# A third buffer for gathered rows, their dots spread over other units, and scatters in another rhythm, in a fused attention and expert-layer block on one core

## The chip, the core and the metric

The kernel runs on one core of a Trainium2 chip. A core has a matrix engine (TensorE, PE in the profile), a vector engine (VectorE, DVE), a scalar engine (ScalarE, ACT), a general engine that also issues indirect transfers (GpSimd, POOL) and a queue engine that issues plain transfers (SyncE, SP). Sixteen DMA engines move the data of both. The metric is the time of one launch on the device, in microseconds (us), as the median of several runs.

## What is computed

One layer on 512 tokens of width 2048 in float32: a mixer (eight forgetting-attention heads, eight stick-breaking heads) and then an expert layer, in which each token picks 128 of 16,384 experts. The part that matters here is the expert layer:

```python
def peer_ffn(xn, w_pq, sub_keys, u, v):
    ...
    q = (xt @ w_pq).reshape(T, PEER_HEADS, 2, PEER_HALF)
    s = jnp.einsum('thcd,hcnd->thcn', q, sub_keys, ...)
    s1, i1 = lax.top_k(s[:, :, 0], PEER_TOPK)
    s2, i2 = lax.top_k(s[:, :, 1], PEER_TOPK)
    cand = (s1[..., :, None] + s2[..., None, :]).reshape(T, PEER_HEADS, PEER_TOPK * PEER_TOPK)
    ...
    top_s, pos = lax.top_k(cand, PEER_TOPK)
    idx = jnp.take_along_axis(cidx, pos, axis=-1)
    g = jax.nn.softmax(top_s, axis=-1).astype(xn.dtype)
    ...
        ub = u[ib]
        h = jax.nn.gelu(jnp.einsum('ted,td->te', ub, xb), approximate=False)
        vb = v[ib]
        return jnp.einsum('te,ted->td', gb * h, vb)
```

So for each token: 128 rows of `u` are dotted with the token, passed through gelu, multiplied by the 128 gates, and weigh 128 rows of `v`.

## The kernel before

**Dense and sparse tokens.** For most tokens the kernel does not gather. It multiplies all of `u` with the tokens (128 blocks of 128 experts), and later multiplies by a dense gate array that is zero where an expert was not chosen. The tokens are in four blocks of 128 (`TB`). The last block (`DB` = 3) is done wholly by gathers, in the later part of the program. Of block 2, the last 32 tokens (`PT`) and the 16 before them (`PB`) are taken out of the dense product, so that it has a width of 336 columns (`UT`). Their dots with the chosen rows of `u` are the *pair rows* of this change. The 32 tokens times 128 slots are 4096 rows, which make `PN` = 32 gathers of 128 rows of 2048 elements (1 MB); the 16 tokens make `NB` = 16 more.

**The stage.** The prologue has 68 units, numbered k = 0 to 67 (`N_PROUNITS`). Each unit is one block of 128 experts: SP loads 1 MB of `u` into `raw` (L412), ACT copies it to `wh` with rounding (`split_hi`, L420), DVE subtracts to get the rest `wl` (`lo`, L1187), and PE runs 48 matmuls of 336 columns (`gemm`, L440 to L442). ACT then takes the sum out with gelu (L1088), and SP stores it (L668). `raw`, `wh` and `wl` have two buffers each, so the load for unit k+2 waits until `lo` of unit k has run. DVE runs `lo` of unit k+1 in its own step k, first of all things in the step. PE cannot begin a unit before `lo` of that unit.

**What else runs in it.** On DVE, in this order within its step k: `lo`, a one-hot build (`hot`, L1528 and L1541, from step 31 on), a table lookup (`lookup`, L1492 to L1499, four steps for each block of tokens, times in `LOOK_AT`), the dots of pair rows (`pair_dot`, L1566) whose unit in `DOT_UNITS` is k, and other small pieces. From unit 32 (`GATE_FROM`) to 63, PE also runs two gate batches of four small matmuls in each unit (`gate_batch`, L2045), ACT takes them out into `gate_piece` (the first 4096 columns of `arena`), and SP stores this every four units (L699).

**The pair rows.** POOL issues for j = 0 to 47 a gather of 128 rows of `u` (L857) into `pair_rows[j % 2]`, once dot j-2 has run (the semaphore `pair_used`), and behind it a few scatters (`scatter_gate`, L843) which put single gates of block 0 into the dense gate array in memory. There are 128 scatters, and `behind[j]` of them follow gather j; each sixteenth waits until all earlier ones have landed. 52 of them stand behind the last gather. DVE's `pair_dot(j)` waits until gather j has landed, and everything behind it on DVE waits with it. After dot 31, SP copies the 16 tokens into `pair_x` (L686), and after the last dot the results are passed to the gates (`pair_weights`, which must be ready before PE's `turn_pair` ahead of unit 56, `PAIR_TURN`).

**After the prologue** follow 15 groups of eight units and a tail. There each unit still loads 1 MB, and the gathers of token block 3 run in three buffers (L874), with a dot or a weighted sum on DVE for each.

## Time and profile before

| | us |
|---|---|
| median of 3 runs | 3255.59 |
| lowest and highest | 3253.79 and 3257.19 |
| the profiled execution | 3256.15 |
| its span in the trace | 3254.4 |

PE is busy for 98% of the span, DVE 67%, ACT 33%, POOL 37%. The profile lists for each engine how long it was busy, how long it sat idle and what ended the idle time; time during which PE waits in a stage in which PE is otherwise without gaps is time of the whole program. The granted clock of PE is listed per stretch as a share of full speed. In timelines, the first two columns are the start and the length of a piece in us, and the bracket at the end is the idle time of that engine just before it and who ended it.

### The profile page before, as it was taken

How to read it: one execution, taken by the hardware profiler on the slowest of the kernel's cores; microseconds unless marked ns; L12 is line 12 of the kernel's file. 1: busy time of each engine (PE TensorE's matmuls, PEld its weight loads, DVE VectorE, ACT ScalarE, POOL GpSimd, SP SyncE). 2: the span in 40 equal slices, each digit the busy share in tenths (PEclk: the TensorE clock that was granted, in tenths of full speed). 3: DMA queues.
4: the chain of work that ended last, by engine and by line, in shares of the span. 5: the costliest groups of instructions: out<-in, count | busy, mean ns of one | idle time of the engine just before them, and what ended most of it. 6: DMA issues, size and time to landing. Idle time of an engine off the chain costs nothing. (4 is left out here: it accounts for less than half of the span.)

```text
span 3254.4 us, 40279 instructions
## 1 busy us (share of the span) xinstructions
PE 3193.3 (98%) x16407; PEld 2795.1 (86%) x16407; DVE 2190.4 (67%) x2514; ACT 1062.6 (33%) x1060; POOL 1209.4 (37%) x555
## 2 busy tenths in 40 slices
PE   8999999999999998889999999999999999999999
PEld 6887777888878898889999889889989988888887
DVE  3016665113037886667775898888888888888887
ACT  4123333444232232236653232323223322222221
POOL 4433333323433325665684233323323331223212
PEclk9999999999999999989999999999999999999999
DMA  4332222223342257888887989899988998888888
GB/s 150 112 109 88 88 88 88 72 88 114 132 142 97 89 181 271 289 257 272 262 235 272 351 338 344 340 345 345 365 320 332 364 338 314 320 336 340 342 321 318
DMA packets 177973, 778.21 MB, mean 239 GB/s; under 512 B 32944, under 2 KB 83248, under 8 KB 92976
## 3 DMA queue, kind: packets, MB, share of 16 engines
q1 hardware_dynamic: 115648, 457.77, 39.0%
q0 software_dynamic: 62208, 318.86, 27.1%
q8 instruction: 76, 1.25, 0.2%
q14 instruction: 41, 0.34, 0.0%
HBM read 731.10 MB, written 44.40 MB: 238 GB/s over the span
## 5 line engine op out<-in xcount | busy, mean ns | idle before, releaser
L440 PE MATMUL bank<-xh,wh 128*128 128x336 f32 (+1 forms) x2928 | 1009.2, 345 | 32.9 <-DVE wl L1187 32.9
L420 ACT ACTIVATE wh<-raw 128x2048 fp32r<-128x2048 f32 x343 | 656.1, 1913 | 1051.9 <-PE bank L467 859.1
L442 PE MATMUL bank<-xh,wl 128*128 128x336 f32 (+1 forms) x2928 | 995.3, 340 | 0.0
L441 PE MATMUL bank<-xl,wh 128*128 128x336 f32 (+1 forms) x2928 | 994.1, 340 | 0.0
L1187 DVE TENSOR_TENSOR wl<-raw,wh 128x2048 fp32r<-128x2048 f32 x252 | 576.9, 2289 | 222.6 <-ACT wh L420 222.5
L426 POOL TENSOR_TENSOR wl<-raw,wh 128x2048 fp32r<-128x2048 f32 x92 | 424.5, 4614 | 721.9 <-ACT wh L420 721.8
L440 PEld LDWEIGHTS bank<-xh,wh 128*128 128x128 f32 x2928 | 555.9, 190 | 71.2 <-DVE wl L1187 31.2
L441 PEld LDWEIGHTS bank<-xl,wh 128*128 128x128 f32 x2928 | 556.2, 190 | 35.2 <-issue 1.9
L442 PEld LDWEIGHTS bank<-xh,wl 128*128 128x128 f32 x2928 | 555.1, 190 | 35.1
L465 PE MATMUL bank<-wh,xh 128*128 128x512 f32 x1328 | 516.9, 389 | 0.0
L467 PE MATMUL bank<-wh,xl 128*128 128x512 f32 x1328 | 516.6, 389 | 0.0
L466 PE MATMUL bank<-wl,xh 128*128 128x512 f32 x1328 | 516.6, 389 | 0.0
L874 POOL DMA_INDIRECT arena<-in_u_rows,g_idx x128 | 247.4, 1932 | 454.2 <-DVE acc L1681 227.6
L874 POOL DMA_INDIRECT arena<-in_v_rows,g_idx x128 | 179.7, 1404 | 605.8 <-DVE acc L1681 314.6
L1660 DVE CUSTOM_DVE_ANT_0 arena<-arena 128x2048 f32<-128x2048 f32 x128 | 291.9, 2288 | 55.5 <-DMA arena<-in_u_rows,g_idx 55.3
L1681 DVE SCALAR_TENSOR_TENSOR acc<-arena,acc 128x2048 f32<-128x2048 f32 x128 | 300.5, 2348 | 3.5 <-DMA arena<-in_v_rows,g_idx 0.2
L465 PEld LDWEIGHTS bank<-wh,xh 128*128 128x128 f32 x1328 | 249.3, 188 | 51.9
L466 PEld LDWEIGHTS bank<-wl,xh 128*128 128x128 f32 x1328 | 249.3, 188 | 51.6
L467 PEld LDWEIGHTS bank<-wh,xl 128*128 128x128 f32 x1328 | 249.3, 188 | 51.5
L843 POOL DMA_INDIRECT gate_scratch<-arena x128 | 264.6, 2067 | 57.1 <-issue 37.2
L465 PE MATMUL bank<-wh,gh 128*128 128x512 f32 x720 | 280.6, 390 | 0.9 <-DVE wl L1187 0.9
L467 PE MATMUL bank<-wh,gl 128*128 128x512 f32 x720 | 280.3, 389 | 0.0
(219 smaller groups left out, 2866.3 us busy)
## 6 DMA issues: line engine op xcount, KB each, us to landing
raw<-in_u SPq DMA_DIRECT2D x128, 1024.0 KB, 5.5
raw<-in_v SPq DMA_DIRECT2D x128, 1024.0 KB, 7.3
raw<-in_w_in SPq DMA_DIRECT2D x56, 1024.0 KB, 5.1
arena<-gate_scratch SPq DMA_DIRECT2D x32, 768.0 KB, 9.1
raw<-in_w_out SPq DMA_DIRECT2D x16, 1024.0 KB, 5.1
raw<-in_w_pq SPq DMA_DIRECT2D x16, 1024.0 KB, 4.8
gate_scratch<-arena SPq DMA_DIRECT2D x8, 2048.0 KB, 9.8
act_scratch<-arena SPq DMA_DIRECT2D x68, 168.0 KB
```

Source lines behind the costliest of these rows:

```text
L420: nc.scalar.activation(wh[s][:], raw[s][:], ACT.Copy).then_inc(hi_done, 1)
L426: nc.gpsimd.tensor_tensor(wl[s][:], raw[s][:], wh[s][:].bitcast(F32), ALU.subtract).then_inc(lo_done, 1)
L440: nc.tensor.matmul(dst, w_h[:, c], xh[:, c, 0:width], start=(c == 0), stop=False)
L441: nc.tensor.matmul(dst, w_h[:, c], xl[:, c, 0:width], start=False, stop=False)
L442: last = nc.tensor.matmul(dst, w_l[:, c], xh[:, c, 0:width], start=False, stop=(c == KC - 1))
L465: nc.tensor.matmul(bank[:], a_hi(e)[:, rows_], w_h[:, e], start=begin, stop=False)
L466: nc.tensor.matmul(bank[:], a_hi(e)[:, rows_], w_l[:, e], start=False, stop=False)
L467: mm = nc.tensor.matmul(bank[:], a_lo(e)[:, rows_], w_h[:, e], start=False, stop=end)
L874: nc.gpsimd.indirect_dma_start(out=rows_g[n % ROW_BUFS], out_offset=None, in_=table, in_offset=bass.IndirectOffsetOnAxis(ap=g_idx[:, slot: ...
L1187: nc.vector.tensor_tensor(wl[k % 2][:], raw[k % 2][:], wh[k % 2][:].bitcast(F32), ALU.subtract).then_inc(lo_done, 1)
L1660: nc.vector.tensor_tensor_reduce(out=rows_g[b], in0=rows_g[b], in1=x_tok, scale=1.0, scalar=0.0, op0=ALU.mult, op1=ALU.add, accum_out=dots ...
L1681: nc.vector.scalar_tensor_tensor(out=acc[:, DB, :], in0=rows_g[b], scalar=dots[:, GM + j:GM + j + 1], in1=acc[:, DB, :], op0=ALU.mult, op1 ...
```

## The change

There are three edits, in the stage just described.

1. **A third buffer.** The first 24 pair-row gathers go in turn to three buffers, the new one being columns 2048 to 4095 of `arena`; from gather 24 on there are two, as before. `PAIR_BUF[j]` is the buffer, `PAIR_TURN_OF[j]` its use number, `PAIR_BEFORE[j]` the gather that had it before. A gather now waits for the dot of `PAIR_BEFORE[j]`. ACT waits for dot 23 before it writes `gate_piece`, which covers the third buffer.
2. **Other units.** The second lookup (block 1) moves from steps 24 to 27 to the steps 14, 18, 22 and 26, and the dots move to steps without a lookup. Units of the dots before and after: 2 and 3 in step 12, against 2 in 12 and 3 and 4 in 13; dots 2 to 21 in steps 12 to 23 before, dots 2 to 16 there now; dots 24 to 31 two in each of steps 28 to 31 before, dots 22 to 27 in steps 28 to 31 now and dots 28 to 31 one each in steps 33 to 36. The dots of the 16 tokens (32 to 47) were in steps 33 to 51 and are in 38 to 52. So the steps of SP and ACT that hang on dot 31 and dot 47 come at step 37 instead of 32, and at 53, 55 and 57 instead of 52, 54 and 56.
3. **Scatters.** Behind gathers 4 to 31 stand one and two scatters in turn (42 in all) instead of one, one and two (39 behind gathers 3 to 31), and 49 behind the last gather instead of 52.

```diff
-LOOK_AT = {0: 8, 1: 24, 3: 56}
+LOOK_AT = {0: (8, 9, 10, 11), 1: (14, 18, 22, 26), 3: (56, 57, 58, 59)}
...
-DOT_UNITS = sorted([9, 11] + list(range(12, 24)) + [12, 14, 15, 17, 18, 20, 21, 23] + [24, 26] +
-                   2 * list(range(28, 32)) + [_k for _k in range(33, 52) if _k not in (36, 41, 46)])
+DOT_UNITS = sorted([9, 11, 12, 13, 13, 15, 15, 16, 17, 17, 19, 19, 20, 21, 21, 23, 23, 24, 25, 25, 27, 27, 28, 28,
+                    29, 30, 30, 31] + list(range(33, 37)) + list(range(38, 53)) + [45])
+PAIR_BUF = [_j % 3 if _j < 24 else _j % 2 for _j in range(PN + NB)]
...
-        pair_rows = [acc[:, 1 + b, :] for b in range(2)]
+        pair_rows = [acc[:, 1, :], acc[:, 2, :], at(D, D)]
...
-            behind = [0] * 3 + [1 + (_j % 3 == 0) for _j in range(3, PN)] + [2 + _j % 2 for _j in range(NB - 1)]
+            behind = [0] * 4 + [1 + _j % 2 for _j in range(4, PN)] + [2 + _j % 2 for _j in range(NB - 1)]
...
-                if j >= 2:
-                    pool.wait_ge(pair_used, j - 1)
+                if PAIR_BEFORE[j] >= 0:
+                    pool.wait_ge(pair_used, PAIR_BEFORE[j] + 1)
...
+                        if b == 0:
+                            act.wait_ge(pair_used, max(_j for _j in range(PN) if PAIR_BUF[_j] == 2) + 1)
...
-                dve.wait_ge(pair_gathered[j % 2], 16 * (j // 2 + 1))
+                rows_j = pair_rows[PAIR_BUF[j]]
+                dve.wait_ge(pair_gathered[PAIR_BUF[j]], 16 * (PAIR_TURN_OF[j] + 1))
```

**Order on DVE, steps 12 to 14.** A `TENSOR_TENSOR` into `wl` is `lo`; each dot is two `ISA` rows (the product and sum, and its read-out); `arena<-arena,acc` is a dot from the third buffer. Before:

```order
L1187 TENSOR_TENSOR wl0<-raw0,wh0 128x2048
L1566 ISA acc,arena<-acc 128x2048
L1566 ISA arena 128x1
L1566 ISA acc,arena<-acc 128x2048
L1566 ISA arena 128x1
L1187 TENSOR_TENSOR wl1<-raw1,wh1 128x2048
L1566 ISA acc,arena<-acc 128x2048
L1566 ISA arena 128x1
L1187 TENSOR_TENSOR wl0<-raw0,wh0 128x2048
L1566 ISA acc,arena<-acc 128x2048
L1566 ISA arena 128x1
L1566 ISA acc,arena<-acc 128x2048
```

After (line numbers are those of the changed kernel):

```order
L1192 TENSOR_TENSOR wl0<-raw0,wh0 128x2048
L1572 ISA arena<-arena,acc 128x2048
L1572 ISA arena 128x1
L1192 TENSOR_TENSOR wl1<-raw1,wh1 128x2048
L1572 ISA acc,arena<-acc 128x2048
L1572 ISA arena 128x1
L1572 ISA acc,arena<-acc 128x2048
L1572 ISA arena 128x1
L1192 TENSOR_TENSOR wl0<-raw0,wh0 128x2048
L1497 TENSOR_TENSOR gl<-arena,iota16 128x1024
L1500 TENSOR_TENSOR gl<-gl,arena 128x1024
L1504 TENSOR_REDUCE arena<-gl 128x64
```

Between two `lo` there stood up to two dots in nearly every step; now a step with one dot, one with two, and one with the lookup and no dot follow each other.

**Order on DVE, steps 30 and 31**, where the third buffer is no longer in use. Before, from `lo` of unit 31 (two dots in each step):

```order
L1187 TENSOR_TENSOR wl0<-raw0,wh0 128x2048
L1566 ISA acc,arena<-acc 128x2048
L1566 ISA arena 128x1
L1566 ISA acc,arena<-acc 128x2048
L1566 ISA arena 128x1
L1187 TENSOR_TENSOR wl1<-raw1,wh1 128x2048
L1528 TENSOR_TENSOR gh<-iota128,arena 128x512
L1536 TENSOR_SCALAR arena<-arena 128x128
L1566 ISA acc,arena<-acc 128x2048
L1566 ISA arena 128x1
```

After, from `lo` of unit 31 (dots 25 and 26, then 27):

```order
L1192 TENSOR_TENSOR wl0<-raw0,wh0 128x2048
L1572 ISA acc,arena<-acc 128x2048
L1572 ISA arena 128x1
L1572 ISA acc,arena<-acc 128x2048
L1572 ISA arena 128x1
L1192 TENSOR_TENSOR wl1<-raw1,wh1 128x2048
L1533 TENSOR_TENSOR gh<-iota128,arena 128x512
L1541 TENSOR_SCALAR arena<-arena 128x128
L1572 ISA acc,arena<-acc 128x2048
L1572 ISA arena 128x1
L1524 COPY arena<-bank 128x384
```

One dot has left step 31; step 30 still has two.

**Order on POOL, from the gathers 2 and 3 on**, `L857` and `L860` being gathers and `L843` and `L846` scatters. Before:

```order
L857 DMA acc<-in_u_rows,arena 128x2048 [waits pair_used] x2
L843 DMA gate_scratch<-arena 6291456x1 [waits gwt_done,placed,gates_zeroed]
L843 DMA gate_scratch<-arena 6291456x1
L857 DMA acc<-in_u_rows,arena 128x2048 [waits pair_used]
L843 DMA gate_scratch<-arena 6291456x1
L857 DMA acc<-in_u_rows,arena 128x2048 [waits pair_used]
L843 DMA gate_scratch<-arena 6291456x1
L857 DMA acc<-in_u_rows,arena 128x2048 [waits pair_used]
L843 DMA gate_scratch<-arena 6291456x1 x2
```

After:

```order
L860 DMA arena<-in_u_rows,arena 128x2048
L860 DMA acc<-in_u_rows,arena 128x2048 [waits pair_used] x2
L846 DMA gate_scratch<-arena 6291456x1 [waits gwt_done,placed,gates_zeroed]
L860 DMA arena<-in_u_rows,arena 128x2048 [waits pair_used]
L846 DMA gate_scratch<-arena 6291456x1 x2
L860 DMA acc<-in_u_rows,arena 128x2048 [waits pair_used]
L846 DMA gate_scratch<-arena 6291456x1
L860 DMA acc<-in_u_rows,arena 128x2048 [waits pair_used]
L846 DMA gate_scratch<-arena 6291456x1 x2
```

The third gather has no wait now and goes to `arena`, and two scatters stand behind every second gather.

## Rows read from the trace of the kernel before

**Rows 1.** The page, busy time of the engines.
```profile
PE 3193.3 (98%) x16407; PEld 2795.1 (86%) x16407; DVE 2190.4 (67%) x2514; ACT 1062.6 (33%) x1060; POOL 1209.4 (37%) x555
```

**Rows 2.** Waits of PE: engine, line, released by: us in total, times, longest.
```profile
PE bank L440 <- DVE wl L1187: 32.9, 11, 6.4
```

**Rows 3.** Stretches: length; busy PE, PEld, DVE, ACT, POOL; PE clock; DMA share; GB/s.
```profile
1240.00:1300.00 60.00, 49.00 (x294) 48.08 (x292) 34.17 (x27) 13.52 (x12) 41.83 (x25) 0.91 0.85 297
1300.00:1360.00 60.00, 48.29 (x290) 46.70 (x288) 34.27 (x26) 14.80 (x14) 42.56 (x23) 0.94 0.83 285
...
sum 210.00, PE 172.16 PEld 168.60 DVE 134.85 ACT 50.03 POOL 142.33; mean PE 34.43 PEld 33.72 DVE 26.97 ACT 10.01 POOL 28.47
```

**Rows 4.** Timeline of ACT: L1088 starts when PE ends a unit.
```profile
1233.50 0.45 ACT L1088 ACTIVATE arena<-bank 128x336 f32<-128x336 f32 x1 [5.10 <-PE bank L442]
...
1240.86 0.45 ACT L1088 ACTIVATE arena<-bank 128x336 f32<-128x336 f32 x1 [5.11 <-PE bank L442]
1241.21 1.91 ACT L420 ACTIVATE wh<-raw 128x2048 fp32r<-128x2048 f32 x1
...
1447.37 0.45 ACT L1088 ACTIVATE arena<-bank 128x336 f32<-128x336 f32 x1 [12.01 <-PE bank L442]
...
1475.17 0.45 ACT L1088 ACTIVATE arena<-bank 128x336 f32<-128x336 f32 x1 [0.66 <-PE bank L442]
...
1484.35 0.45 ACT L1088 ACTIVATE arena<-bank 128x336 f32<-128x336 f32 x1 [4.97 <-PE bank L442]
```

**Rows 5.** Timeline of DVE: two `lo` with two late dots between, and a lookup.
```profile
1254.43 2.29 DVE L1187 TENSOR_TENSOR wl<-raw,wh 128x2048 fp32r<-128x2048 f32 x1
1261.20 2.29 DVE L1566 CUSTOM_DVE_ANT_0 acc<-acc 128x2048 f32<-128x2048 f32 x1 [4.49 <-DMA acc<-in_u_rows,arena]
...
1266.30 2.29 DVE L1566 CUSTOM_DVE_ANT_0 acc<-acc 128x2048 f32<-128x2048 f32 x1 [2.80 <-DMA acc<-in_u_rows,arena]
...
1268.52 2.29 DVE L1187 TENSOR_TENSOR wl<-raw,wh 128x2048 fp32r<-128x2048 f32 x1
...
1371.90 1.22 DVE L1492 TENSOR_TENSOR gl<-arena,iota 128x1024 fp32r<-128x1024 f32 x1
```

**Rows 6.** Timeline of POOL in the same stretch, and one scatter that waited.
```profile
1250.37 2.81 POOL L857 DMA_INDIRECT acc<-in_u_rows,arena  x1 [1.50 <-DVE arena L1566]
...
1256.26 1.33 POOL L857 DMA_INDIRECT acc<-in_u_rows,arena  x1 [0.30 <-issue]
...
1407.51 1.57 POOL L843 DMA_INDIRECT gate_scratch<-arena  x1 [4.13 <-DMA gate_scratch<-arena]
```

**Rows 7.** DMA from 1250 to 1440: packets, MB, engine share; issues to landing, us.
```profile
q0 software_dynamic: 9529, 29.87, 45.3%
q1 hardware_dynamic: 5472, 23.19, 35.3%
...
raw<-in_u SPq DMA_DIRECT2D x19, 1024.0 KB, 5.3
...
gate_scratch<-arena POOLq DMA_INDIRECT x38
acc<-in_u_rows,arena POOLq DMA_INDIRECT x28, 8.3
```

**Rows 8.** DMA from 1610 to 1735, where POOL issues 48 scatters alone.
```profile
q0 software_dynamic: 7243, 0.25, 11.8%
```

**Rows 9.** A stretch of the later groups, columns as in rows 3.
```profile
2100.00:2300.00 200.00, 200.00 (x1078) 181.36 (x1078) 175.19 (x106) 57.92 (x45) 61.71 (x39) 1.00 0.92 350
```

**Rows 10.** POOL's last gather and last scatter, and the queue engine behind it.
```profile
1602.09 1.21 POOL L857 DMA_INDIRECT acc<-in_u_rows,arena  x1 [1.65 <-DVE arena L1566]
...
1735.93 3.29 POOL L843 DMA_INDIRECT gate_scratch<-arena  x1 [0.30 <-issue]
...
1754.04 0.33 SPq L412 DMA_DIRECT2D raw<-in_u  x1
```

**Rows 11.** Start of unit 54 by ACT, and the end of `pair_weights` on DVE.
```profile
1640.29 0.45 ACT L1088 ACTIVATE arena<-bank 128x336 f32<-128x336 f32 x1 [0.71 <-PE bank L442]
...
1647.73 0.29 DVE L1581 TENSOR_TENSOR arena<-arena 64x128 f32<-64x128 f32 x1
```

More of the change, by code:

```diff
@@ L382, in build @@
         pair_chosen = sem("pair_chosen")
-        pair_gathered = [sem(f"pair_gathered{b}") for b in range(2)]
+        pair_gathered = [sem(f"pair_gathered{b}") for b in range(3)]
         pair_used = sem("pair_used")
@@ L1613, in _ @@
                 for t in LOOK_AT:
-                    if LOOK_AT[t] <= k < LOOK_AT[t] + 4:
-                        lookup(t, (k - LOOK_AT[t]) // 2, (k - LOOK_AT[t]) % 2)
-                if k == LOOK_AT[0] + 3:
+                    if k in LOOK_AT[t]:
+                        lookup(t, LOOK_AT[t].index(k) // 2, LOOK_AT[t].index(k) % 2)
+                if k == LOOK_AT[0][-1]:
                     place()
```

12 lines of the change are left out of this document (7 added, 5 removed).

## The prediction

> **What bounds the kernel now.** I read the page first. PE is busy for 98% of the span [rows 1], so the program is as long as PE's work plus PE's gaps, and another engine matters only where PE waits for it. Then the waits of PE. Only one of them is long and lies in the stage of the change: 32.9 us, in 11 pieces, before the first matmul of a unit, released by DVE's `lo` [rows 2]. Then the stretches of that stage. From 1240 to 1450 PE is busy for 172.2 of 210 us and its granted clock is between 0.78 and 0.94 of full speed [rows 3]; later, in the main groups, it is busy for 200 of 200 at 1.00 [rows 9]. So time is lost in two ways, and I count both at once by the length of the units. ACT's L1088 marks the end of a unit. An undisturbed unit is 1240.86 - 1233.50 = 7.36 us, one with gate batches 1484.35 - 1475.17 = 9.18. Units 13 to 32 run from 1240.86 to 1447.37 [rows 4], which is 206.5 us; without a disturbance they would take 19 x 7.36 + 9.18 = 149.0. The loss is **57.5 us**: 210 - 172.2 = 37.8 idle, the rest clock. All other units of the prologue that I looked at have their undisturbed length within a few tenths.
>
> Why `lo` is late stands in DVE's timeline. Between the `lo` at 1254.43 and the next at 1268.52 lie two dots that waited 4.49 and 2.80 us for their gathers [rows 5]. POOL's timeline gives the round trip: the gather issued at 1250.37 was used at 1261.20, the one of 1256.26 at 1266.30, so 10 to 11 us from issue to use [rows 5, 6]. A buffer's cycle is then about 0.3 (dot to issue) + 10 + 2.3 (dot) = 12.6 us. With two buffers that is a dot each 6.3 us, but the old table asks for 20 dots in the 12 units 12 to 23, one each 88.3 / 20 = 4.4 us.
>
> **The change, part by part.** *Third buffer with the new units.* Three buffers allow a dot each 12.6 / 3 = 4.2 us. The new table asks for 26 dots in the 20 units 12 to 31, one each 147.2 / 26 = 5.7. Does each step fit on DVE? `lo` can start 2.35 after its unit's start (L1088 and L420 on ACT [rows 4]) and DVE needs about 2.2 to 2.3 for `lo` and for each dot [rows 5]. A step with two dots ends at 2.3 + 3 x 2.2 = 9.0, which is 1.6 into the next unit, and the next `lo` may begin as late as 5.1 into it. So a two-dot step bears some 3.4 us of waiting for gathers before PE notices, a one-dot step 5.6. A lookup step has no dot: 2.3 + 2.2 + 3 x 1.25 = 8.3 [rows 5], which fits. Walking through the steps with these numbers and with POOL's mean of (41.83 + 42.56) / 48 = 1.76 us for an instruction [rows 3] plus its gap of 0.3 [rows 6], no dot before 23 waits longer than 1.7 us, and nothing reaches PE.
>
> The end of the three-buffer part is different. Count from the start of unit 28. Gather 23 starts near 0 (after dot 20), and dot 23 waits until 9.9, ends 12.1. Gather 24 starts at 5.9, behind 23 and two scatters, and dot 24 ends at 18.2, with `take_slots` at 18.8. Gather 25 starts at 10.0. Gather 26 needs the buffer of dot 24 (two buffers now) and also stands behind scatter 32, the one that waits for all earlier scatters; such a wait was 4.1 us at 1407.51 [rows 6]. It starts at 19.7 and lands at 29.7. In step 30 `lo` runs to 21.1, dot 25 to 23.4, and dot 26 waits 6.3 us and ends at 32.0. So `lo` of unit 32 ends at 34.2 where PE wants it at 29.4: **about 5 us are left**. The same walk through the old table gives 54 us of lateness, against 57.5 measured, which is why I trust it.
>
> *DMA load.* Take shares of 16 engines. From 1250 to 1440, q1 used 35.3% of 190 us for 19 units, 3.53 us a unit; q0 used 45.3%, 86.1 us, for 28 gathers and 38 scatters [rows 7]. A scatter is 11.8% of 125 us / 48 = 0.31 [rows 8], so a gather is (86.1 - 11.7) / 28 = 2.66. Units 12 to 31 now need 20 x 3.53 + 23 gathers (5 to 27) x 2.66 + 35 scatters x 0.31 = 142.6 us in 147.2, or 97%. The later groups run at a share of 0.92 with PE never waiting [rows 9]; at such a share the 142.6 take 155, which is 8 us too long. The stretch now runs at 0.83 to 0.85 [rows 3], with pauses since the gathers wait for buffers. Between 5 (no crowding) and 8 to 9 (a share of 0.92), I take **8 us left**, nearer to the loaded end, since the rows of the later groups are the ones with three buffers.
>
> *Clock.* The clock was 1.00 where PE had no gaps [rows 9] and lower only where it had. It is inside the 57.5 and goes with it; with 5 us of stall left some of it stays, inside the 8.
>
> *Scatters and the tail.* POOL has 49 scatters behind the last gather instead of 52, but that gather comes one unit later. The 52 took from 1603.3 to 1739.2 [rows 10], 2.6 us each; so the tail ends, seen from the units, 9.2 - 3 x 2.6 = 1.4 us later. SP's load behind it was issued at 1754.04 [rows 10], and that was due to `lo`; 15 us of cover, 13.6 now: nothing. All of it shifts with the units, as it hangs on dots.
>
> *Steps that move on SP and ACT.* `pair_weights` ended 1647.73 + 0.3 - 1640.29 = 7.7 us into unit 54 [rows 11]; the same work in unit 55 must be done at its end, 9.2, where PE's `turn_pair` now waits for it: 1.4 us of cover, and if it fails, as much is lost as it is late; I take 0, bound 2. The copy of the 16 tokens (eight small transfers) comes at SP's step 37, behind a 2 MB gate store, and is wanted a unit later: 0, bound 2. ACT's new wait is for dot 23 (step 28) at step 33: 0.
>
> Sum: 57.5 - 8 = 49.5 us gained. The profiled execution had 3256.15, so 3206.7; the median of the runs is 0.6 below it: **3206**. Nothing behind the prologue changes, as its groups start from the same order of events.
>
> Two rules of the Trainium skill can be set beside this. Rows first: a gather's landing took 8.3 us in the median [rows 7]. The skill's page "DMA: Bandwidth & Descriptors", section "Anatomy of one DMA — SWDGE (gpsimd) path", fits 2.0 us plus bytes / 436e3 us, an estimate of 4.4 us for 1 MB. By that a third buffer would hardly be needed and the loss would be some 14 us, not 57.5; the measured landing decides. If that is what an unloaded gather takes, the other 4 us are queueing, which more gathers in flight may lengthen: the second case below. And the gather that started within `lo` took 2.81 us on POOL, one beside it 1.33 [rows 6]. "SBUF — State Buffer", section "Who interferes with whom", infers that a `tensor_tensor` doesn't hold up descriptor generation; the row speaks against that. By the page POOL would be some 2 us less late; the sum has the measured mean.
>
> **The rivals.** *Forecast* (0.66): 2 to 15 us left, 3199 to 3214; the low end is 57.5 with only 2 left, the high end 8, the two bounds of 2 of the moved steps and 3 for one more late step.
>
> *DMA or POOL is full* (0.19): at the share seen now, 0.85, the 142.6 us take 168, 20 too long; with the stall of 5 that leaves 15 to 28: 3214 to 3227. For it: 97% is more than any long row shows, and POOL's 2.5 instructions for each dot are 5.2 us of 5.7. Against: gathers 24 to 27 are all that must be on time at the end, and three early gathers are a reserve.
>
> *The third buffer gives nothing* (0.09): say gathers of one queue are served strictly one behind the other, so that the cycle stays at 12.6 for two. The new units alone then leave stalls of about 5 us in each group of four units (19, 23, 27) and 5 + 2 + 5 in 30 to 32, with small ones some 33 us, at a trip of 11 us 43: 3230 to 3241. Against: in the later groups 350 GB/s are moved with three buffers of the same kind [rows 9].
>
> *The stall is not the dots* (0.03), and PE waits again for late loads of `u`: loads landed in 5.3 us [rows 7] and have some 10; within 0.2%.
>
> *Slower* (0.03): the tail of scatters becomes what starts the main groups. Dense gathers fill POOL, the prologue is 49.5 us shorter, and if scatters slow from 2.6 us to over 4.0 each, 49 of them eat the cover of 13.6 and the gain and 6.5 more: 3262 and up. The tail's rate was steady in its two rows, so little.
>
> **How the numbers follow.** A measurement of this kernel can tell 0.2%, 6.5 us. The range goes from the forecast's low end to nearly the end of the second case, 3199 to 3226; about 0.85 lies within, and leaving out the second case would leave 0.34 out. Faster is the first three cases, 0.94; same 0.03; slower 0.03.
>
> **What would show it.** In the changed profile units 13 to 31 should be 7.36 long and PE's wait before L443 a few us, nearly all at unit 32 (and perhaps 30), released by `lo`, with DVE waiting for gather 26. The clock from 1240 on should be 1.00 but near that place. DMA share there should be 0.9 or more, and landing of gathers 9 to 12 us. Landing over 12, or stalls at 15, 19, 23 and 27, would be the second or third case; a wait before `turn_pair`, or of SP for `scattered` ahead of the main groups, would show that moved steps had no cover.

## The result

The changed kernel takes 3228.18 us (median of 4 runs, 3225.24 to 3236.83) against 3255.61 for the kernel before: a ratio of 0.9918 with an interval of 0.9906 to 0.9931. That is 27 us faster. The forecast was 49.5 us faster, with a range that ended at 3226, so the result lies 2 us outside it. The direction was right; almost half of the expected gain is missing. Section by section below, "loss" is counted as in the prediction: the length of a stretch of units, read from ACT's L1091 (L1088 before), less 7.36 us for each plain unit and 9.175 for each with gate batches.

The profiled execution took 3236.83 us, the slowest of the four. The page's line of busy times, which answers to [rows 1]:

```profile
PE 3188.1 (99%) x16407; PEld 2791.3 (86%) x16407; DVE 2189.6 (68%) x2514; ACT 1062.4 (33%) x1060; POOL 1233.8 (38%) x555
```

Waits of PE over the whole program (engine, line, released by: us in total, times, longest), as [rows 2]. The wait for `lo` fell from 32.9 to 18.0 us, and one for the one-hot build ahead of a gate batch rose from 3.8 us to 6.7:

```profile
PE bank L443 <- DVE wl L1192: 18.0, 5, 6.4
...
PE bank L2051 <- DVE arena L1546: 6.7, 2, 3.7
```

Stretches of the stage, columns as in [rows 3] (length; busy PE, PEld, DVE, ACT, POOL; clock; DMA share; GB/s). The last row is the start of the main groups:

```profile
1240.00:1300.00 60.00, 60.00 (x393) 60.00 (x392) 51.02 (x38) 18.05 (x16) 51.01 (x24) 1.00 0.95 329
1300.00:1360.00 60.00, 57.78 (x368) 57.50 (x367) 45.21 (x35) 18.05 (x16) 48.92 (x26) 0.97 0.95 318
1360.00:1410.00 50.00, 42.61 (x271) 42.03 (x271) 32.73 (x37) 14.09 (x18) 35.05 (x17) 0.93 0.86 285
...
1500.00:1550.00 50.00, 46.28 (x313) 46.00 (x312) 35.18 (x54) 26.56 (x42) 41.05 (x17) 0.97 0.79 252
1550.00:1600.00 50.00, 47.00 (x318) 46.72 (x316) 36.89 (x58) 27.72 (x38) 40.33 (x17) 0.97 0.92 286
1731.20:1800.00 68.80, 60.42 (x310) 55.24 (x309) 43.98 (x29) 18.65 (x15) 15.86 (x12) 0.93 0.88 333
```

The first 60 us, where PE lost 11 us and its clock was 0.91 before, now run without a gap at 1.00, as forecast. POOL is busy there for 51.01 of 60 us in 24 instructions. With 0.3 us ahead of each, that is 58 of 60: **POOL is full**. The gaps of PE lie in three other places. ACT's timeline gives their size, as [rows 4] (the ends of units 12, 32 and 67, then ACT's first copy of the main groups, which waited for its load):

```profile
1243.20 0.46 ACT L1091 ACTIVATE arena<-bank 128x336 f32<-128x336 f32 x1 [5.10 <-PE bank L445]
...
1406.66 0.45 ACT L1091 ACTIVATE arena<-bank 128x336 f32<-128x336 f32 x1 [5.61 <-PE bank L445]
...
1731.14 0.45 ACT L1091 ACTIVATE arena<-bank 128x336 f32<-128x336 f32 x1 [5.28 <-PE bank L445]
1735.99 1.92 ACT L423 ACTIVATE wh<-raw 128x2048 fp32r<-128x2048 f32 x1 [4.40 <-DMA raw<-in_u]
```

Units 13 to 32 took 1406.66 - 1243.20 = 163.5 us, a loss of 14.5 (57.5 before): 4.0 at unit 27 and 10.5 in units 28 to 32. Units 33 to 67 lost 10.6 (1.4 before). From the end of unit 67 (1762.64 before) to the end of the span it is 3235.1 - 1731.14 = 1504.0 us, against 3254.4 - 1762.64 = 1491.8. With 2.3 us that unit 12 ended later (1243.20 against 1240.86; unit 0 was already that late, and no other profile shows it), the difference of the two profiled executions is 43.0 - 9.2 - 12.2 - 2.3 = 19.3 us, which is 3256.15 - 3236.83. In a second profile of the same kernel (a_rep, 3231.78) it is 41.3 - 7.5 - 9.5 + 0.1 = 24.4.

**Place one, units 27 to 32.** Unit 27 is late through dot 19, which still has three buffers. POOL's gather 19, then its dot and `lo` of unit 27 on DVE:

```profile
1335.04 1.94 POOL L860 DMA_INDIRECT acc<-in_u_rows,arena  x1 [0.30 <-issue]
```

```profile
1343.87 2.29 DVE L1572 CUSTOM_DVE_ANT_0 acc<-acc 128x2048 f32<-128x2048 f32 x1 [3.21 <-DMA acc<-in_u_rows,arena]
...
1346.09 2.28 DVE L1192 TENSOR_TENSOR wl<-raw,wh 128x2048 fp32r<-128x2048 f32 x1
```

Units 30 to 32 are late through dot 26. DVE's timeline: dots 25 and 26, then `lo` of unit 32.

```profile
1379.86 2.29 DVE L1572 CUSTOM_DVE_ANT_0 acc<-acc 128x2048 f32<-128x2048 f32 x1
...
1390.66 2.29 DVE L1572 CUSTOM_DVE_ANT_0 acc<-acc 128x2048 f32<-128x2048 f32 x1 [8.50 <-DMA acc<-in_u_rows,arena]
...
1392.88 2.29 DVE L1192 TENSOR_TENSOR wl<-raw,wh 128x2048 fp32r<-128x2048 f32 x1
```

POOL's timeline there: gather 25, scatters 31 and 32 (the latter waits until all earlier ones have landed, as at 1407.51 in [rows 6]), gathers 26 and, one scatter further, 27.

```profile
1369.83 2.67 POOL L860 DMA_INDIRECT acc<-in_u_rows,arena  x1 [0.30 <-issue]
1372.80 2.48 POOL L846 DMA_INDIRECT gate_scratch<-arena  x1 [0.30 <-issue]
1382.70 1.56 POOL L846 DMA_INDIRECT gate_scratch<-arena  x1 [7.42 <-DMA gate_scratch<-arena]
1384.57 1.00 POOL L860 DMA_INDIRECT acc<-in_u_rows,arena  x1 [0.30 <-issue]
...
1387.75 1.00 POOL L860 DMA_INDIRECT acc<-in_u_rows,arena  x1 [0.30 <-issue]
```

Dot 26 is late, as the prediction said, but its gather was used 6.1 us after its start (1384.57 to 1390.66). It was late because it started late, behind a wait for landing of 7.42 us where the walk had 4.1. Counted as in the walk, from the start of unit 28 (1357.56 here), gather 25 started at 12.3 instead of 10.0 and gather 26 at 27.0 instead of 19.7. Of these 7.3 us, 3.3 are the longer wait, 2.3 the later gather 25, and the rest longer instructions between them. Its buffer had been free since 1377.1, the end of dot 24.

**Place two, units 46 to 48.** Again DVE (two dots in step 45, the second waiting 7.90 us) and POOL (its gather at 1519.62):

```profile
1521.84 2.29 DVE L1572 CUSTOM_DVE_ANT_0 acc<-acc 128x2048 f32<-128x2048 f32 x1
...
1532.04 2.29 DVE L1572 CUSTOM_DVE_ANT_0 acc<-acc 128x2048 f32<-128x2048 f32 x1 [7.90 <-DMA acc<-in_u_rows,arena]
```

```profile
1513.91 3.54 POOL L846 DMA_INDIRECT gate_scratch<-arena  x1 [0.30 <-issue]
1517.76 1.56 POOL L846 DMA_INDIRECT gate_scratch<-arena  x1 [0.30 <-issue]
1519.62 2.58 POOL L860 DMA_INDIRECT acc<-in_u_rows,arena  x1 [0.30 <-issue]
1522.50 3.07 POOL L846 DMA_INDIRECT gate_scratch<-arena  x1 [0.30 <-issue]
1525.88 1.56 POOL L846 DMA_INDIRECT gate_scratch<-arena  x1 [0.30 <-issue]
...
1533.13 2.67 POOL L846 DMA_INDIRECT gate_scratch<-arena  x1 [4.38 <-DMA gate_scratch<-arena]
```

The buffer was free at 1515.91 (the dot of 1513.69 and its read-out), POOL came to the gather 3.7 us later, and its rows were used after 12.4 us.

**Place three, the start of the main groups.** POOL's longest wait for landing, its last scatter, the first instruction behind the wait for all of them, and SP's load for the second main unit, which waits for the same (1754.04 in [rows 10]):

```profile
1653.09 2.42 POOL L846 DMA_INDIRECT gate_scratch<-arena  x1 [12.55 <-DMA gate_scratch<-arena]
...
1727.01 2.61 POOL L846 DMA_INDIRECT gate_scratch<-arena  x1 [0.30 <-issue]
1731.15 0.26 POOL L870 MEMSET arena<- 128x192 f32 x1 [1.53 <-DMA gate_scratch<-arena]
```

```profile
1731.16 0.33 SPq L415 DMA_DIRECT2D raw<-in_u  x1
```

Before, that load went out 8.6 us ahead of the end of unit 67. Now it leaves with that end, 0.01 us after the row in which POOL goes on because all scatters have landed, and PE waits twice in 1700 to 1800, 8.4 us in all.

### The profile page after: what moved, and what is told of

The parts are those of the page before. It is cut to its first block, busy times and chain, and to the rows that moved or that the text cites. A ratio compares the mean times of both kernels' runs of the same rounds, so it can differ in the third digit from the quotient of the medians.

```text
span 3235.1 us, 40279 instructions
## 1 busy us (share of the span) xinstructions
PE 3188.1 (99%) x16407; PEld 2791.3 (86%) x16407; DVE 2189.6 (68%) x2514; ACT 1062.4 (33%) x1060; POOL 1233.8 (38%) x555
## 4 chain that ended last, share of the span: by engine, by line
PE 89%; DMA 4%; POOL 3%; DVE 1%; ACT 1%; issue 1%; SPq 0%; ACTq 0%; DVEq 0%
PE bank L468 14%; PE bank L469 14%; PE bank L470 14%; PE bank L443 14%; PE bank L445 14%; PE bank L444 14%; POOL gate_scratch L846 3%; DMA raw<-in_u 1%; PE bank L2051 1%; PE bank L1882 1%; DMA gate_scratch<-arena 1%; POOL acc L860 1%; PE bank L1863 1%; DMA acc<-in_u_rows,arena 1%; PE bank L1927 1%
## 5 line engine op out<-in xcount | busy, mean ns | idle before, releaser
L443 PEld LDWEIGHTS bank<-xh,wh 128*128 128x128 f32 x2928 | 553.9, 189 | 54.9 <-DVE wl L1192 11.1
L846 POOL DMA_INDIRECT gate_scratch<-arena x128 | 287.0, 2242 | 78.1 <-DMA gate_scratch<-arena 41.3
```

What stands on the lines that cost most here:

```text
L443: nc.tensor.matmul(dst, w_h[:, c], xh[:, c, 0:width], start=(c == 0), stop=False)
L846: nc.gpsimd.indirect_dma_start(out=gate_cells, out_offset=bass.IndirectOffsetOnAxis(ap=where[:, j:j + 1], axis=0), in_=best[:, 0].rearrang ...
```

## The experiments

All times are medians of four runs or more, and each ratio is to the kernel before, run in the same set. The theory after the first profile: the third buffer and the new units do what they should, and what is left comes from POOL, whose queue of gathers and scatters is full. Rivals: the two-buffer round trip of gather 26 (the prediction's step), DMA engines that are full, the dots of the 16 tokens being too close by themselves, and, for the start of the main groups, the 3 MB reload of `acc`.

This table has the readings of all profiles (one for each kernel), worked out as above: losses in units 13 to 32 and 33 to 67, how long before the end of unit 67 the last scatter started, and the time from that end to the span's end ("rest"). "Late" is how much later than in the kernel before the fourth unit of the main groups ended, counted from the end of unit 67. It is the part of "rest" that the start of the main groups costs. The time of before is from its set in the first row, and it was 3256.6 to 3258.3 in the other four.

| kernel | median us | 13 to 32 | 33 to 67 | last scatter | late | rest |
|---|---|---|---|---|---|---|
| before | 3255.6 | 57.5 | 1.4 | 26.7 | 0 | 1491.8 |
| changed | 3228.2 | 14.5 | 10.6 | 4.1 | 12.8 | 1504.0 |
| a_rep | 3231.2 | 16.2 | 8.9 | 13.9 | 4.7 | 1501.3 |
| b_buf | 3238.2 | 34.1 | 0.1 | 26.7 | 0.0 | 1494.5 |
| c_units | 3250.4 | 31.5 | 10.2 | 4.1 | 12.0 | 1504.1 |
| d_noscat | 3205.2 | 0.7 | 0.1 | | 0.0 | 1499.6 |
| e_oldscat | 3224.4 | 4.9 | 8.6 | 4.1 | 12.6 | 1508.4 |
| f_buf27 | 3226.7 | 15.9 | 8.3 | 14.0 | 5.2 | 1497.8 |
| g_scatmove | 3216.6 | 6.9 | 8.2 | 14.0 | 4.4 | 1496.3 |
| h_both | 3215.2 | 5.1 | 8.9 | 12.3 | 4.6 | 1500.5 |
| k_thin | 3227.1 | 8.3 | 2.8 | 1.3 | 14.7 | 1507.6 |
| l_late | 3225.6 | 9.2 | 6.0 | 1.1 | 14.4 | 1508.4 |
| m_poolbusy | 3202.2 | 7.9 | 0.6 | | 0.0 | 1492.9 |
| n_tail8 | 3220.9 | 15.0 | 7.9 | 32.3 | 0.0 | 1492.9 |

The two last columns don't always go together. In d_noscat the main groups begin on time, and yet "rest" is 7.8 us longer than before; in a_rep, e_oldscat and h_both some 4 to 5 us of it aren't late starts. That time is lost inside the main groups. In d_noscat its largest piece stands at the very end:

```profile
3150.00:3203.90 53.90, 47.02 (x195) 37.97 (x193) 39.04 (x25) 7.76 (x5) 9.24 (x6) 0.93 0.78 287
```

In the last 53.9 us of the kernel before PE was busy for 50.54 at a clock of 0.99. What causes this loss stays open.

### The changed kernel again

> The changed kernel once more, unaltered, for a second trace. Theory A, three fixed places: the loss of some 37 us that the first trace shows (units 27 and 30 to 32: 14.5; units 46 to 48: 10.4; the start of the main groups behind the last scatters: 12.3) comes from the order of the work, so a second trace shows a loss at the same three places, each within about 5 us, and the ratio to before is 0.989 to 0.994. Theory B, chance: the places differ from run to run (transfers that collide by chance), so that at least one of the three is gone and the time is nearer to 3225 than to 3237.

Measured: 3231.24 us (3224.22 to 3237.18), ratio 0.9918 [0.9894, 0.9943]. The losses are much the same: 5.1 at units 25 and 27 (behind dots 16 and 19, which waited 5.52 and 6.17 us), 11.1 in units 28 to 32, 8.9 about unit 46. Only the start of the main groups differs more than the 5 us allowed (4.7 us late instead of 12.8), with a last scatter that came 10 us earlier.

### One edit at a time: the buffer, the units

b_buf keeps the old units, lookups and scatters and has the third buffer alone. c_units has the new units with two buffers and the old scatters. In c_units:

```diff
-PAIR_BUF = [_j % 3 if _j < 24 else _j % 2 for _j in range(PN + NB)]
+PAIR_BUF = [_j % 2 for _j in range(PN + NB)]
```

> The third buffer alone: the old units of lookups and dots, the old rhythm of scatters. Theory A (a buffer's round trip of 12.6 us bounds the dots): the walk through the steps leaves 25 to 29 us of lateness in units 13 to 32 instead of 57.5, so 3224 to 3232 if nothing is lost behind it, and up to 12 more where the last scatters reach the main groups. Rival C (the third buffer gives nothing, gathers of one queue are served one behind the other): 3250 to 3257.

> The new units of lookups and dots alone: two buffers and the old rhythm of scatters. Theory A: with a trip of 10 to 11 us the walk leaves 33 to 43 us in units 13 to 32, with stalls of about 5 us at 19, 23, 27 and 30 to 32: 3231 to 3241 and a little more for the tail. Rival C: the units are the whole of the change, so this one is as fast as the changed kernel, 3225 to 3230.

Measured: b_buf 3238.22 us, ratio 0.9943 [0.9926, 0.9961]; c_units 3250.44, 0.9971 [0.9957, 0.9985]. Of the 57.5 us in units 13 to 32, the buffer alone takes 23.4, the units alone 26.0, both together 43.0, and both with the old scatters (e_oldscat, below) 52.6. Each half is worth something, and neither makes up for the other. This refutes the rival "the third buffer gives nothing": without it the new units keep 31.5 us of loss, with it 14.5, and b_buf is far from that rival's 3250 to 3257. Both expectations missed in part: b_buf kept 34.1 us instead of 25 to 29, and c_units kept less than the 33 to 43 expected but took 9 us more than 3241, since nothing had been counted for units 33 to 67 and too little for the tail. The other columns tell what the new units cost: the loss of some 10 us in units 46 to 51 and the late start of the main groups come with the new units even at the old scatter rhythm (c_units), and are absent without them (b_buf). So c_units gains 26 us and gives back about 21.

### No scatters

The 128 scatters and all waits for them are left out (the gates of token block 0 stay zero).

```diff
-                for slot in range(sum(behind[:j]), sum(behind[:j + 1])):
-                    scatter_gate(slot)
...
-            pool.wait_ge(scattered, 16 * SLOTS)
```

> The changed kernel without the 128 scatters and without the waits for them; the gates of token block 0 stay zero, so this work is left out. Theory A (POOL, whose scatters stand ahead of gathers, makes the dots late at units 27, 30 to 32 and 46 to 48, and the last scatters hold up the main groups): the loss at 46 to 48 and at the main groups goes, and that at 27 to 32 falls to 5 or less: 3198 to 3206. Rival B2 (the DMA engines are full at those places; a scatter is only 0.3 us of them): units 27 to 32 and 46 to 48 still lose some 20 us together and only the start of the main groups is mended: 3212 to 3218.

Measured: 3205.22 us (3203.93 to 3206.28), ratio 0.984 [0.9823, 0.9856]. The stretches of d_noscat:

```profile
1240.00:1400.00 160.00, 160.00 (x1056) 159.97 (x1055) 131.72 (x113) 55.35 (x62) 55.37 (x27) 1.00 0.89 339
1500.00:1600.00 100.00, 100.00 (x700) 100.00 (x699) 76.12 (x122) 63.07 (x94) 8.94 (x8) 1.00 0.77 273
```

PE has no gap in the prologue, at 339 GB/s against 329 and 318 in the changed kernel. So gathers, loads of `u` and dots fit, and the losses of the prologue and the late main groups hang on the scatters. A DMA share that is full by gathers and loads is refuted. That the time is the predicted one (3205.2, forecast 3206) is luck: the prologue lost 0.8 us where the forecast had left 8, and the main groups lost 7.8 us where it had nothing.

### POOL busy, but nothing moved

Each scatter is replaced by four fills of 128x512 on POOL, one after the other (again the gates of block 0 stay zero).

```diff
-                    scatter_gate(slot)
+                    for step in range(4 * slot, 4 * slot + 4):
+                        if step:
+                            pool.wait_ge(pool_step, step)
+                        nc.gpsimd.memset(gl[:, 1024:1536].bitcast(F32), 0.0).then_inc(pool_step, 1)
```

> The changed kernel with each of its 128 scatters replaced by four fills of 128 x 512 numbers on POOL, one after the other, which keep POOL busy for about 2.1 to 2.6 us, nearly as long as a scatter (2.24 us and a gap of 0.3), but move nothing; the gates of token block 0 stay zero, and nothing waits for landed scatters. It stands between the changed kernel (3228 to 3231, losses 14 to 16 in units 13 to 32 and 9 to 11 in 33 to 67) and d_noscat (3205, losses 0.7 and 0.1). If POOL's issue time alone is what makes the gathers late, the losses should be 8 to 16 and 5 to 10, and the time 3218 to 3230. If the waits for landed scatters (3.8 to 12.6 us, seven of them) and the traffic of the scatters do it, the losses should be under 3 and 2, and the time 3205 to 3210.

Measured: 3202.19 us (3199.05 to 3207.04), ratio 0.9829 [0.9812, 0.9845]. The groups of POOL's fills in m_poolbusy and of its scatters in the changed kernel (busy us, mean ns | idle before them):

```profile
L870 POOL MEMSET gl<- 128x512 f32 x512 | 273.0, 533 | 26.9
```

```profile
L846 POOL DMA_INDIRECT gate_scratch<-arena x128 | 287.0, 2242 | 78.1 <-DMA gate_scratch<-arena 41.3 <-issue 36.9
```

The fills take 300 us with their gaps, the scatters 324 without their waits for landing, so POOL's load is nearly the same. The result falls between the two theories. In units 13 to 32 the loss is 7.9 us, all at unit 31: dot 26 waits 4.2 us, and its gather began straight behind fills. That is the 5 to 8 us which the prediction had for this place, and POOL's issue time accounts for it. In 33 to 67 it is only 0.6 us. The rest, some 7 us in 13 to 32 (the 4 to 5 at units 25 and 27 among it), 8 to 10 in 33 to 67, and the late main groups, needs what the fills don't have: the waits for landing (41.3 us in all) and scatters whose length goes up to 6.32 us. These two were not separated. Nor does the median show the 7.9 us, since it is 3 us below that of d_noscat. The two profiles say why that can be: m_poolbusy lost 7.8 us more in the prologue, but its main groups took 6.7 us less (1492.9 against 1499.6). Its profiled execution was also the longest of its four.

### A third buffer for longer

Gathers 24 to 26 stay in the turn of three, so gather 26 no longer waits for a dot two places ahead of it.

```diff
-PAIR_BUF = [_j % 3 if _j < 24 else _j % 2 for _j in range(PN + NB)]
+PAIR_BUF = [_j % 3 if _j < 27 else (_j - 27) % 2 for _j in range(PN + NB)]
```

> The changed kernel with the third buffer kept for gathers 24 to 26 too; from 27 on two buffers. Gather 26 then waits for dot 23 and not for dot 24. Theory A (the loss of some 10 us at units 30 to 32 is the round trip of gather 26 in two buffers): that stall goes to 3 us or less, the time falls by 6 to 10 us against the changed kernel. Rival A2 (gather 26 is late since POOL comes to it late, behind scatters and the wait at scatter 32): the stall stays at 7 us or more, and the time is within 3 us.

Measured: 3226.68 us (3223.91 to 3229.71), 0.9905 [0.9888, 0.9921], not to be told from the changed kernel. Its timelines of POOL and of DVE, at the same place:

```profile
1381.15 2.92 POOL L846 DMA_INDIRECT gate_scratch<-arena  x1 [5.45 <-DMA gate_scratch<-arena]
1384.37 1.01 POOL L860 DMA_INDIRECT arena<-in_u_rows,arena  x1 [0.30 <-issue]
```

```profile
1390.16 2.29 DVE L1572 CUSTOM_DVE_ANT_0 arena<-arena,acc 128x2048 f32<-128x2048 f32 x1 [7.52 <-DMA arena<-in_u_rows,arena]
```

Gather 26 now goes to the third buffer, starts at the same time as before, and its dot waits 7.52 us. The buffer was not what it waited for; the scatter ahead of it was, with its wait for landing. Units 28 to 32 lose 8.3 us instead of 10.5 and 11.1, so the two buffers are worth 3 us there at most. The prediction had both causes in its walk, and there too the scatter's wait ended last; but it took the change from three buffers to two for what makes this place different, and that is refuted. What the two buffers would do comes next in line: in g_scatmove, below, gather 26 waits 5.21 us for dot 24, whose buffer it takes.

### The scatters elsewhere

e_oldscat is the changed kernel with the old rhythm (edit 3 undone: 52 behind the last gather). g_scatmove takes six scatters away from gathers 23 to 27 and four from 34 to 46, and puts the ten behind 28 to 33, where POOL waits for dots; 79 stay ahead of the last gather. h_both is g_scatmove and f_buf27 together.

```diff
-            behind = [0] * 4 + [1 + _j % 2 for _j in range(4, PN)] + [2 + _j % 2 for _j in range(NB - 1)]
+            behind = [0] * 4 + [1 + _j % 2 for _j in range(4, 23)] + [0, 1, 0, 1, 0] + [3] * 5 + [6] + \
+                [3 if _j in (36, 42) else 2 for _j in range(34, PN + NB - 1)]
```

> The changed kernel with the old rhythm of scatters (39 behind gathers 3 to 31 and 52 behind the last, as before the change). The runs so far: without scatters the prologue loses nothing, with them 25 us, and some 5 to 12 more at the start of the main groups. Theory A2 (POOL is nearly full, so a few scatters more or less behind each gather only move the lateness about): within 4 us of the changed kernel either way, less late in units 27 to 32 by 1 or 2 us and the tail of scatters up to 8 us later, so more lost at the main groups. Rival (the rhythm is what carries the change): 8 us slower or more.

> The changed kernel with the same count of scatters ahead of the last gather (79) in another rhythm: 2 instead of 8 behind gathers 23 to 27, 21 instead of 11 behind gathers 28 to 33, where POOL sat idle, and 28 instead of 32 behind gathers 34 to 46. Theory A2 (POOL's queue is what makes the dots late): the stall at units 30 to 32 falls to about half and the one at 46 to 48 too, 6 to 12 us less than the changed kernel. Theory A (round trip in two buffers): the first stall stays, 0 to 4 us less.

> Both of the last two edits: the third buffer up to gather 26 and the moved scatters. Theory A and A2 together: units 13 to 37 lose 3 us or less, units 38 to 63 half of the 9 to 10 us, the main groups still 5 to 12: 3208 to 3218, faster than the changed kernel by 10 to 18 us. If one of the two theories is wrong, it is as the better one of the two single edits.

Measured: e_oldscat 3224.35 us (3217.91 to 3227.79), 0.9892 [0.9875, 0.9908]; g_scatmove **3216.57** (3211.26 to 3219.95), 0.9872 [0.9856, 0.9889]; h_both **3215.23** (3207.9 to 3219.92), 0.9863 [0.9846, 0.9879]. DVE of g_scatmove at dot 26 (the wait was 8.50), and PE's wait for `lo` in 1240 to 1410 (9.6 us in the changed kernel):

```profile
1381.71 2.29 DVE L1573 CUSTOM_DVE_ANT_0 acc<-acc 128x2048 f32<-128x2048 f32 x1 [2.94 <-DMA acc<-in_u_rows,arena]
```

```profile
PE bank L443 <- DVE wl L1193: 3.5, 1, 3.5
```

Moving these scatters by a few gathers about halves the loss in units 13 to 32, from 14.5 and 16.2 (15.0 in n_tail8) to 6.9 (8.3 and 9.2 in k_thin and l_late, which have the same scatters there), with buffers and units untouched. That is more than the 6 to 12 us expected of the whole. The loss in 33 to 67, which should have halved too, did not: 8.2 us, most of it at unit 41 instead of 46. The intervals of g_scatmove and h_both lie below both of the changed kernel; whether h_both is better than g_scatmove can't be told. Its time came as expected, its places didn't (5.1 us in 13 to 32 where 3 or less was expected, 8.9 behind them where half of that was). e_oldscat shows that edit 3 was no help to the dots: without it units 13 to 32 lose only 4.9 us, where 1 or 2 us less than the changed kernel had been expected. Three more scatters stand in its tail, but its main groups start no later than those of the changed kernel (12.6 us, against 12.8); another 4 us of its "rest" are lost inside the groups. The median is not to be told from the changed kernel.

### Units 46 to 48, and the tail

k_thin is g_scatmove with 20 instead of 28 scatters behind gathers 34 to 46, and so 57 behind the last. l_late is k_thin with the 3 MB reload of `acc` at SP's step 62 instead of 57. n_tail8 is the changed kernel with its last 8 scatters left out (their gates stay zero).

```diff
-                [3 if _j in (36, 42) else 2 for _j in range(34, PN + NB - 1)]
+                [1 if _j in (36, 38, 39, 40, 41, 42) else 2 for _j in range(34, PN + NB - 1)]
```

```diff
-                if k == DOT_UNITS[-1] + 5:
+                if k == 62:
```

```diff
-                for slot in range(sum(behind[:j]), sum(behind[:j + 1])):
+                for slot in range(sum(behind[:j]), min(sum(behind[:j + 1]), SLOTS - 8)):
```

> The kernel of g_scatmove with 20 scatters instead of 28 behind gathers 34 to 46, so that 57 instead of 49 stand behind the last gather. There is left a loss of 8 to 9 us at unit 41 or 46. Theory P: POOL is full there, since a dot's share of 1 gather and 2.2 scatters of 3 us takes as long as a unit; units 33 to 67 should then lose 3 us or less instead of 8.2. Rival D: the DMA engines are full there (share 0.97 in 1500 to 1580), or 16 dots in 15 units do not fit by themselves; then the 8 us stay. Price under either: 8 more scatters of 2.7 us in the tail, 21.6 us, less the 8 that the last gather comes earlier; the last scatter stood 14.0 us ahead of the end of unit 67, so it comes about with it, and the main groups may start some 5 us late. Total: P 3210 to 3218, D 3217 to 3226.

> The kernel of k_thin with SP's 3 MB reload of acc at step 62 instead of 57. In the profile of the changed kernel a wait of POOL for landed scatters was 12.55 us at 1653, behind that reload and a 2 MB gate store. Theory T: the reload holds the scatters' landing up; that wait should be 4 to 7 us, the last scatter 5 to 8 us earlier against the end of unit 67, and the main groups start without a gap (PE idle before the first main matmul under 2 us): 3205 to 3213. Rival: the gate store alone, or the collision of the reload with later waits, does it; the last scatter stands where it does in k_thin, and the time is that of k_thin within 3 us.

> The changed kernel with the last 8 of its 128 scatters left out (those experts' gates of token block 0 stay zero), so that 41 instead of 49 stand behind the last gather; everything ahead of that gather is as in the changed kernel. Theory: the last scatter starts the main groups, since SP's load for the second main unit waits until all have landed. In the changed kernel it was issued 4.1 and 13.9 us ahead of the end of unit 67 and the first main groups began 10.5 and 2.8 us late; in b_buf it was 26.7 us ahead and nothing was late. Here it should be 24 to 34 us ahead, the main groups begin within 0.5 us of their place and the program take 4 to 12 us less than the changed kernel, 3217 to 3226, with the losses in the prologue as they were (13 to 17 and 8 to 11 us). Rival: the main groups begin late for another reason (the 3 MB reload, late activations); then they are still 3 to 12 us late and the time is 3226 to 3232.

Measured: k_thin 3227.08 us (3224.31 to 3230.69), 0.9912 [0.9895, 0.9929]; l_late 3225.64, 0.9899 [0.9882, 0.9916]; n_tail8 3220.88 (3218.54 to 3221.55), 0.9883 [0.9867, 0.99].

k_thin: theory P's reading came in its profile (2.8 us instead of 8.2 in units 33 to 67), but l_late, with the same scatters, lost 6.0 there, all at unit 41 and ahead of the step that was moved. So thinning helped by 2 to 5 us in these profiles, and one profile doesn't tell how much. Rival D falls by d_noscat and m_poolbusy, which have the same dots and lose 0.1 and 0.6. The total missed: 3210 to 3218 was expected. The last scatter started 1.3 us before the end of unit 67, and the main groups began 14.7 us late instead of the "some 5" that I had allowed. A scatter taken out of the gathers' way is paid in the tail.

l_late: the time is as the rival said, that of k_thin within 3 us, and the last scatter comes at the same place (1.1). But the long wait moved with the reload. In k_thin the reload left at 1623.41, and the wait of 10.02 us began 10.4 us behind it. In l_late the wait about that place took 1.80 us, and the one of 11.08 us stands right behind the reload's new place. POOL, then SP, of l_late:

```profile
1639.74 1.55 POOL L846 DMA_INDIRECT gate_scratch<-arena  x1 [1.80 <-DMA gate_scratch<-arena]
...
1684.62 1.65 POOL L846 DMA_INDIRECT gate_scratch<-arena  x1 [11.08 <-DMA gate_scratch<-arena]
```

```profile
1671.93 0.43 SPq L698 DMA_DIRECT2D acc<-acc_scratch  x1
```

The other profiles agree. In the changed kernel, c_units and e_oldscat too, the wait that began 1 to 7 us behind the reload took 12.55, 10.91 and 10.88 us, and no other scatter behind the last gather waited over 7.5. In a_rep POOL came to it 2.8 us ahead of the reload, and it took 5.79: most of the 10 us by which a_rep's last scatter was earlier. So the reload does go with the long landing. Why landings take longer there stays open, and no run shows a reload placed where no group of scatters is waited for.

n_tail8 is the counterpart: the same losses in the prologue (15.0 and 7.9), but SP's load leaves 8.7 us ahead of the end of unit 67 at 1726.81, as in the kernel before, and the first main groups begin where they should, within 0.1 us. So the last scatters cause the late start. Its timeline of SP:

```profile
1718.08 0.33 SPq L415 DMA_DIRECT2D raw<-in_u  x1
```

How much cover the tail needs can be read from a_rep. Its last scatter started at 1714.80 and ran for 1.56 us, and then its POOL and SP had these rows:

```profile
1721.07 0.26 POOL L870 MEMSET arena<- 128x192 f32 x1 [4.72 <-DMA gate_scratch<-arena]
```

```profile
1721.08 0.33 SPq L415 DMA_DIRECT2D raw<-in_u  x1
```

The last scatter landed 4.7 us after its issue had ended, the load left 7.6 us ahead of the end of unit 67 (1728.70) instead of 8.6, and PE waited 2.9 us (with the clock that this costs, 4.7 us late).

A version with fewer waits for landing was not tried. Each such wait stands between two heads' gates, two heads can pick the same expert, and their scatters would then add to one cell while both are in flight.

## Why the prediction was right and wrong

- **What bounds the kernel, and the third buffer with the new units: right in the main.** Up to unit 26 the changed kernel lost nothing, in its first profile, and PE's clock went back to 1.00 there. Without scatters the prologue lost 0.8 us.
- **"No dot before 23 waits longer than 1.7 us, and nothing reaches PE" was wrong.** Dot 19 waited 3.21 us and unit 27 took 4.0 us more (in a_rep dots 16 and 19 waited 5.52 and 6.17, and units 25 and 27 took 5.1 us more). All profiles with new units, third buffer and scatters lose 4 to 8 us at these two units; d_noscat and m_poolbusy lose nothing there. The step behind it is POOL's queue, taken at its mean.
- **The term of the sum that failed: "8 us left" in units 13 to 32, which measured 14.5 and 16.2.** At the end of the three-buffer part place and dot were right (26, in step 30). The size was off, 10.5 and 11.1 us in units 28 to 32 where the walk had 5, and so was the weight of the causes: not the two-buffer round trip (f_buf27), but POOL's queue. Its issue time alone makes 7.9 us (m_poolbusy). The wait for landing ahead of scatter 32, taken at 4.1 us from the one row of such a wait [rows 6], measured 7.42, 6.27 and 5.45 in three profiles (2.43 in e_oldscat, where units 28 to 32 lost 0.9). I had one row for it and took it as the value, though it varies by 5 us. That the 8 us had been raised from 5 for a crowded DMA brought the number nearer by luck: d_noscat shows no such crowding.
- **POOL priced as a mean.** I put POOL's load (2.5 instructions per dot, "5.2 us of 5.7") into a rival and not into the sum. That is 91% of the time, before any wait for landing, and leaves no reserve; g_scatmove and e_oldscat show 8 to 11 us hanging on where a few scatters stand. And the mean of 1.76 us hid two kinds of rows. In the prologues of all the profiles together, 870 scatters that began outside DVE's instructions of 2.3 us (`lo`, dots) took 1.57 us in the median, and 658 that began within one took 3.01: none of these ended less than 1.4 us after that instruction of DVE, most 1.45. For gathers it is 1.01 against 2.58 us, none ending less than 0.8 us after it. So a part of POOL's load is set by what DVE does beside it; no run changed that alone.
- **Units 33 to 67: put at nothing, without a reason.** The dots of the 16 tokens went from 19 steps to 15, and I costed only the steps of SP and ACT. A dot there brings 2.5 scatters and a gather; with the lengths of 1.6 to 4.1 us seen around 1520 that comes near to the unit of 9.2. It cost 9.2 and 7.5 us.
- **The tail: "15 us of cover, 13.6 now: nothing" was wrong.** It cost 12.8 and 4.7 us. Three things were left out. The last scatter must also land, 1.5 to 4.7 us after its issue. The last gather did not come 9.2 us but 19.8 us later, seen from the end of unit 67 (160.6 us ahead of it before, 140.8 now): 5.9 of the 10.6 come with the new units even without scatters (145.5 in d_noscat), the rest since POOL had fallen behind. And 49 scatters took 136 us instead of 127, with one wait of 12.55 behind the reload. Together 1.5 + 10.6 + 9 = 21 of the 13.6 + 8.6 = 22.2 us that the prediction left between the last scatter and the end of unit 67, where the load did leave. The mechanism stood in the prediction, as the "slower" rival, with a far too high threshold (scatters of over 4.0 us).
- **DMA load: right for a wrong place.** The share was 0.95 as foreseen (0.9 or more), but d_noscat moved 339 GB/s at 0.89 without a gap, more than the 329 and 318 of the changed kernel. So the "DMA or POOL is full" rival, whose range 3214 to 3227 the result nearly met, was half right: POOL, not the DMA engines' gathers and loads. That its number nearly fitted is luck, as it was worked out from the DMA share alone.
- **pair_weights, the copy of the 16 tokens, ACT's new wait: right at nothing.** PE waited for nothing between 1580 and 1700 (units 51 to 63), in any profile but that of c_units, where it waited once for a one-hot build.
- **The two rules of the Trainium skill.** Where a dot waited for it, a gather of the changed kernel was used 5.6 to 13.2 us after its start, so the row, not the estimate of 4.4 us by the fit of the Trainium skill's page "DMA: Bandwidth & Descriptors", was the one to go by; that the fit holds for an unloaded chip no run here shows. And m_poolbusy, where POOL has no scatters, repeats the other row. The gather at 1280.48 lay beside `lo` and the first instruction of the lookup, both of them a `tensor_tensor`, and took 2.71 us; the one at 1256.20 began 0.4 us before DVE fell idle and took 0.95. In the prologues of all profiles, none of the gathers that began within a `lo` ended less than 0.8 us after that `lo`. The inference of the Trainium skill's page "SBUF — State Buffer", section "Who interferes with whom", does not hold for this kernel. POOL, then DVE:

```profile
1256.20 0.95 POOL L860 DMA_INDIRECT acc<-in_u_rows,arena  x1 [0.15 <-issue]
...
1280.48 2.71 POOL L860 DMA_INDIRECT arena<-in_u_rows,arena  x1 [0.15 <-issue]
```

```profile
1255.36 1.22 DVE L1508 TENSOR_REDUCE arena<-gl 128x64 f32<-128x1024 f32 x1
1258.07 2.29 DVE L1196 TENSOR_TENSOR wl<-raw,wh 128x2048 fp32r<-128x2048 f32 x1 [1.49 <-ACT wh L424]
...
1280.08 2.29 DVE L1196 TENSOR_TENSOR wl<-raw,wh 128x2048 fp32r<-128x2048 f32 x1 [0.65 <-ACT wh L424]
1282.29 1.22 DVE L1501 TENSOR_TENSOR gl<-arena,iota 128x1024 fp32r<-128x1024 f32 x1
```

## What to carry to other kernels

When a dependency is relieved, cost the next queue at its fullest, instruction by instruction, and not at its mean: an engine that issues transfers for two purposes and is 90% full is the new bound. Where one issue stream has urgent and unurgent work, the place of a few unurgent ones can be worth more than half of a buffer (12 to 15 us here, for one line, against 20 for the third buffer alone). And a tail that runs beside other work has a deadline: find the first instruction that waits for it, and count the landing, and every delay of the tail's start, against its cover. A time that comes out as forecast proves little by itself: look whether it is made up of the terms that were forecast (d_noscat's was not).

## What was not expected of the hardware

- A wait for landed scatters of 128 single numbers took 0.4 to 7.6 us in most places, but 10.0 to 13.2 us in nine. All nine began 1 to 10 us behind one of two transfers of SP: the 3 MB reload of `acc` (five) or the eight small copies of the 16 tokens (four: 11.28, 12.45, 13.18 and 11.05 us in g_scatmove, h_both, k_thin and l_late). Moving the reload moved the wait. The copies were not moved, so for them it isn't shown.
- The same scatter takes 1.56 us on POOL or anything up to 6.32 (6.49 in the kernel before), mostly by whether it began within a long instruction of DVE, as told above. The fills of 128x512 took 0.53 us in the mean, and four or eight of them in a row 2.3 and 4.6 to 4.8 us throughout the prologue, beside DVE's work or not.
